# Attention's score matmuls in bursts of four, and the mixer's norms with squares added up on VectorE

## The reference

```python
u = rms_norm(h, norm_mix)
q, k, v, xl, gl = split(u @ w_in)            # 512 | 128 | 128 | 512 | 512 columns
q, k = rope(rms_norm(q)), rope(rms_norm(k))  # 8 query heads, 2 kv heads of 64
attn_out = softmax(q k^T / 8) v              # all 2048 keys, no mask
lru_out = (scan_forward + scan_backward)(conv(xl)) * gelu(gl)
mixed = concat(rms_norm(attn_out), rms_norm(lru_out))
h = h + mixed @ w_out
u = rms_norm(h, norm_ffn)
h = h + (silu(u @ w_gate) * (u @ w_up)) @ w_down    # 2816 wide
```

## Time and profile before

| | us |
|---|---|
| median of 3 runs | 2062.04 (2061.69 to 2065.15) |
| profiled execution, device time | 2065.6 |
| its span, slowest core (7) | 2064.1 |
| its span, fastest core (1) | 2040.4 |
| TensorE busy in it | 1836.4 |
| ScalarE / VectorE / GpSimd busy | 1070.5 / 933.8 / 348.9 |

### The profile page before, as it was taken

How to read it: one execution, slowest core, us unless ns; L and a number is a source line. 1 busy time by engine, 2 the same in 40 slices (tenths; PEclk the granted TensorE clock), 3 DMA queues, 4 the chain that set the end, 5 groups by cost and what they waited for, 6 DMA issues and landing times.

```text
span 2064.1 us, 24894 instructions; the slowest of 8 cores (2040.4 to 2064.1 us)
## 1 busy us (share of the span) xinstructions
PE 1836.4 (89%) x8272; PEld 727.3 (35%) x8272; DVE 933.8 (45%) x1159; ACT 1070.5 (52%) x1340; POOL 348.9 (17%) x380
## 2 busy tenths in 40 slices
PE   4994567865679999999999999999999999999998
PEld 1441223311112233333333344444444444444443
DVE  1666999856782221112141233353433534434331
ACT  3666888788988877877788711120211301213010
POOL 1223554445431122201000000000000000000000
PEclk9996778978889999999999999999999999999999
DMA  8653342481228465526642248567476575574632
GB/s 176 194 163 113 115 135 92 157 208 56 72 70 219 119 151 132 127 78 156 163 140 63 66 147 255 178 183 243 142 224 209 148 257 152 156 221 133 201 116 97
DMA packets 139784, 310.99 MB, mean 151 GB/s; under 512 B 18544, under 2 KB 26864, under 8 KB 139664
## 3 DMA queue, kind: packets, MB, share of 16 engines
q1 hardware_dynamic: 111632, 228.55, 37.9%
q0 software_dynamic: 28032, 80.86, 14.8%
HBM read 263.05 MB, written 69.99 MB: 161 GB/s over the span
## 4 chain that ended last, share of the span: by engine, by line
PE 69%; DVE 10%; DMA 9%; issue 5%; ACT 4%; POOL 2%; SPq 1%; DVEq 0%; POOLq 0%; ACTq 0%
PE ps_all L479 52%; PE ps_all L755 10%; PE ps_all L718 6%; DMA arena<-xT 2%; DVE arena L826 2%; DVE arena L790 2%; DMA arena<-rs_d 1%; DMA xl_d<-arena 1%; ACT arena L723 1%; DVE arena L572 1%; DMA arena<-xl_d 1%; DMA arena<-wd_s 1%; DMA arena<-w_out 1%; ACT arena L803 1%; DMA arena<-q_d 1%
## 5 line engine op out<-in xcount | busy, mean ns | idle before, releaser
L479 PE MATMUL ps_all<-arena 128*128 128x512 bf16 (+1 forms) x6224 | 1447.9, 379 | 149.1 <-ACT arena L803 27.3
L479 PEld LDWEIGHTS ps_all<-arena 128*128 128x128 bf16 x6224 | 609.1, 100 | 865.2 <-issue 262.0
L723 ACT ACTIVATE arena<-ps_all 128x1024 bf16<-128x1024 f32 x512 | 517.9, 1034 | 121.5 <-PE ps_all L755 102.5
L976 ACT ACTIVATE arena<-ps_all 128x512 f32<-128x512 f32 x176 | 104.6, 596 | 604.6 <-PE ps_all L479 604.3
L755 PE MATMUL ps_all<-arena 128*65 128x512 bf16 x1024 | 400.2, 408 | 6.4 <-DVE arena L731 6.3
L978 DVE SCALAR_TENSOR_TENSOR arena<-arena,ps_all 128x512 f32<-128x512 f32 x176 | 120.7, 687 | 365.2 <-ACT arena L976 364.5
L718 PE MATMUL ps_all<-arena 64*128 64x512 bf16 x1024 | 207.8, 402 | 63.2 <-ACT arena L723 57.3
L1001 POOL DMA_DIRECT2D outT<-arena x64 | 34.6, 540 | 997.0 <-DVE arena L999 996.4
L755 PEld LDWEIGHTS ps_all<-arena 128*65 128x65 bf16 x1024 | 107.8, 112 | 178.5 <-issue 133.0
L981 DVE SCALAR_TENSOR_TENSOR arena<-arena,ps_all 128x512 bf16<-128x512 f32 x176 | 120.9, 687 | 107.8 <-PE ps_all L479 104.6
L718 PEld LDWEIGHTS ps_all<-arena 64*128 64x128 bf16 x1024 | 51.2, 93 | 283.7 <-issue 283.7
(11 more groups left out here) (59 smaller groups left out, 894.6 us busy)
## 6 DMA issues: line engine op xcount, KB each, us to landing
arena<-wg_s SPq DMA_DIRECT2D x154, 256.0 KB, 3.0
arena<-wu_s SPq DMA_DIRECT2D x154, 256.0 KB, 2.9
arena<-wd_s SPq DMA_DIRECT2D x56, 704.0 KB, 5.8
arena<-xT SPq DMA_DIRECT2D x64, 512.0 KB, 7.1
outT<-arena POOLq DMA_DIRECT2D x64, 256.0 KB, 6.1
arena<-wo_s SPq DMA_DIRECT2D x56, 256.0 KB, 2.9
xl_d<-arena POOLq DMA_DIRECT2D x32, 256.0 KB, 3.6
gl_d<-arena POOLq DMA_DIRECT2D x32, 256.0 KB, 3.5
```

The source lines that it names most:

```text
L479: P.op("pe", lambda e: e.matmul(t.ap(n) if ap is None else ap(t), lhsT=lhsT, rhs=rhs, start=start, stop=stop), reads=reads, writes=[t], co ...
L723: P.op("act", lambda e: e.activation(out=pb, in_=T.ap(1024), func=AF.Exp, scale=0.125), reads=[T], writes=[("Pb", si % 3)], cost=c_act(102 ...
L976: P.op("act", lambda e, G=G, b=b: e.activation(out=tg[b], in_=G.ap(), func=AF.Tanh, scale=0.5), reads=[G], writes=[("tg", b)], cost=c_act( ...
```

## The change

Three things change.

- Attention: `emit_qk` takes a count m. With m = 2 it is one operation of four matmuls, into S0 and S1, that needs both PSUM tiles, and the two exponentials follow. In the first sequence this holds from step 192 on (`NS0`), in the second from its third step on. There are four `Pb` buffers for three.
- Norms of stage D: `sum_sq` squares in f32, adds the squares up on VectorE one after the other, the last sum in bf16, and one matmul with ones gives the sum over partitions. The buffers are now `hsq` (f32, two), `acc` and `accb` (one each), and `rf` has one buffer for two. The last addition of a chunk is written over h, which the store reads, instead of to a buffer `ot`.
- The planner: its costs for ScalarE, TensorE and DMA are others, it counts 0.1 us at each change between 64-row and other matmuls (`half`), and S0, S1 and O have one queue for both sequences.

```diff
-        q = P.bank_queue.setdefault((P.stream, kind), [])
+        q = P.bank_queue.setdefault((P.stream if kind == "m" else "B", kind), [])
...
+            if e == "pe":
+                if o["half"] != halved:
+                    cost += 0.1
+                halved = o["half"]
...
-                ch = 1 if o["eng"] == "pool" else 0
-                f = max(s + cost + 2.0, dma_free[ch]) + o["nbytes"] / 180e3
-                dma_free[ch] = f - 1.0
+                dma_free = max(s + cost + 0.9, dma_free) + o["nbytes"] / 200e3
+                f = dma_free + 1.2
...
-    return 0.04 + n / 1200.0 + 0.09 * ptrs
+    return 0.085 + n / 1200.0 + 0.09 * ptrs
...
-    return 0.0025 + n / 2400.0
+    return 0.006 + n / 2400.0
...
-                T = Bank(P, "S%d" % (si % 2), 2)
-
-                def both(e):
-                    for u in range(2):
-                        rows = slice(64 * u, 64 * u + 64)
-                        r = e.matmul(T.ap(1024)[:, u * 512:(u + 1) * 512], lhsT=kT[sq][rows, stl * 128:(stl + 1) * 128],
-                                     rhs=qb[n % 2][rows, :], start=True, stop=True)
+                T2 = [Bank(P, "S%d" % ((si + i) % 2), 2) for i in range(m)]
+
+                def burst(e):
+                    for i in range(m):
+                        for u in range(2):
+                            rows = slice(64 * u, 64 * u + 64)
+                            kt = (stl + i) * 128
+                            r = e.matmul(T2[i].ap(1024)[:, u * 512:(u + 1) * 512], lhsT=kT[sq][rows, kt:kt + 128],
+                                         rhs=qb[n % 2][rows, :], start=True, stop=True)
                     return r
-                P.op("pe", both, reads=[("k", sq, stl // 4), ("qb", n % 2)], writes=[T], cost=0.25, lat=0.25)
+                P.op("pe", burst, reads=[("k", sq, stl // 4), ("qb", n % 2)], writes=T2, cost=0.03 + 0.217 * m,
+                     lat=0.25, half=True)
...
-            for si in range(len(steps)):
+            emit_qk(0, 1)
+            emit_qk(1, 1)
+            for si in range(0, len(steps), 2):
+                two = si + 2 >= single
                 if si + 2 < len(steps):
-                    emit_qk(si + 2)
+                    emit_qk(si + 2, 2 if two else 1)
                 emit_pv(si)
+                if si + 2 < len(steps) and not two:
+                    emit_qk(si + 3, 1)
+                emit_pv(si + 1)
...
+        def sum_sq(N, parts, eng):
...
+            for n, (ap, key) in enumerate(parts):
+                sb = dc["s"] % 2
+                dc["s"] += n > 0
+                dst, dkey = (acc[a], ("acc", a)) if n == 0 else (hsq[sb], ("hsq", sb))
...
+                if n:
+                    o, okey = (accb[a], ("accb", a)) if n == last else (acc[a], ("acc", a))
+                    P.op("dve", lambda e, o=o, sb=sb: e.tensor_tensor(out=o, in0=acc[a], in1=hsq[sb], op=ALU.add),
+                         reads=[("acc", a), ("hsq", sb)], writes=[okey], cost=c_dve(512))
+            mm(N, ones_bf, accb[a], True, True, ["cm", ("accb", a)])
...
-            for k in range(8):
-                sb = dc["s"] % 2
-                dc["s"] += 1
-                P.op("act", lambda e, k=k, sb=sb: e.activation(out=hsq[sb], in_=h[:, k, :], func=AF.Square),
-                     reads=[("h", hb, k)], writes=[("hsq", sb)], cost=c_act(512), lat=0.25)
-                mm(N, ones_bf, hsq[sb], k == 0, k == 7, ["cm", ("hsq", sb)])
-            r = dc["r"] % 2
+            sum_sq(N, [(h[:, k, :], ("h", hb, k)) for k in range(8)], "act")
+            r = dc["r"] % len(rf)
```

83 lines of the change are left out of this document (43 added, 40 removed).

## The result

| | before | after |
|---|---|---|
| median of 4 runs each, us | 2062.28 (2061.69 to 2065.15) | 2010.62 (2007.97 to 2011.83) |
| ratio of the times, 95% interval | | 0.9745 (0.9728 to 0.9762) |
| span of the slowest core, us | 2064.1 | 2010.3 |
| mean over the cores: step 192 starts, us | 735.3 | 729.0 |
| last score pair | 1171.9 | 1206.5 |

A step's start is that of its first score matmul, and the matmuls of stage D are the helper's (line 483, 479 before) less the 1360 of stages A and C.

A forecast was written before the change was run, and what follows sets the result against it. TensorE was taken to bound the kernel, above 97% busy from some 700 us on. Terms -22.6 - 33.4 + 21 + 8 + 3 = -24 us took the profiled 2065.6 to 2041.6, less 3.6 for the median: 2038 us, range 2014 to 2058.

The forecast's parts named there:

- norms, 104 matmuls: Stage D: 16 ones-matmuls per chunk become 3, so 104 matmuls at 0.2178 us go, 22.6 us less.
- changes of shape, 159: Attention from step 192 on: 159 bursts each save one change of matmul shape and back, 0.21 us, 33.4 us less.
- waits, step 192 to 511: Attention bursts: TensorE waits 21 us for a 2.85 us ScalarE loop, plus 8 us for added changes of table.
- stage D's waits: Stage D: weights through GpSimd's queue, taken faster by D now, were costed at nothing, 0 us.
- up to step 192, matmuls of D credited: Before step 192: six more changes of table, two where ScalarE is full, cost +3 us, with 12 us allowed either way.
- I cost it at nothing: Stage D norms: a chain 2 to 5 us longer is covered by 38 us of down-projection or gate and up matmuls.
- TensorE's few waits from 745 us on: Old TensorE waits from 745 us on, 1.8 us of them for the exponential, were left as they are.
- 1225: Milestone: the last score pair comes near 1225 us for 1180.6, with 3621 helper matmuls behind it for 3998.
- A: Attention bursts: ScalarE's loop is longer than its parts, 3.2 us, and sets the pace; 2078 us; chance 0.09.
- B: Attention bursts: the second pair starts no closer than after a change of shape, nothing of 33.4 comes; 2060 us; chance 0.06.
- C: Attention from step 192: the loop is 2.8 us and the tables hide; -38, 2024 us; chance 0.18.
- D: First third: it loses 15 us or more by its new order; 2053 us and up; chance 0.09.

The follow-up runs named there:

- e1_norms: The kernel before with the change of the norms alone, old attention and old planner costs kept; ratio 0.9945 to the kernel before.
- e9_olddma: The changed kernel with the planner's old model of DMA time alone put back; ratio 0.9962 to the kernel before.
- e15_oldrear: The changed kernel planned with new costs up to step 96 of the first sequence and old ones from there; ratio 0.9836 to the kernel before.
- e13_oldnorms: The changed kernel with the old norms (16 ones-matmuls per chunk), bursts and planner costs kept; ratio 0.9856 to the kernel before.
- e5_pb4: The kernel before with a fourth probability buffer alone and one rstd buffer instead of two; ratio 1.0016 to the kernel before.
- e3_plan: The kernel before with the planner's new costs and common bank queue alone, old attention and norms; ratio 0.9977 to the kernel before.
- e7_pb3: The changed kernel with three probability buffers instead of four; ratio 0.9895 to the kernel before.
- e14_oldfront: The changed kernel planned with old costs up to step 96 of the first sequence and new ones from there; ratio 0.9772 to the kernel before.
- e6_exp768: The changed kernel, same queues, with each attention exponential doing 768 of the 1024 columns; ratio 0.9661 to the kernel before.

## Why the prediction was wrong

The account of the 52.1 us on the mean core, beside the forecast:

| term | forecast | measured |
|---|---|---|
| norms, 104 matmuls | -22.6 | -22.5 |
| changes of shape, 159 | -33.4 | -35.6 |
| waits, step 192 to 511 | +21 + 8 | +19 |
| stage D's waits | 0 | -4.2 |
| up to step 192, matmuls of D credited | +3 | -9.8 |
| not explained, behind step 511 | | +1 |
| sum | -24 | -52 |

(From step 192 to 511: +40.8 = 266 more matmuls of D x 0.2165 - 159 x 0.224 + 18.8. The waits counted one by one give 31.1 - 11.4 = 19.7, 1 more. Behind: -86.6 = 386 fewer matmuls x 0.2165, 4.2 of waits, 1.2 the other way. Up to step 192: -6.3, with 16 more matmuls of D done.)

Three terms failed, and all to the same side: what moves before step 192 (13 us of the 28 missed), the waits of the bursts (10) and stage D's waits (4); the changes of shape add 2.

**Norms.** Right in size. VectorE got 13 x 0.692 and, for its 8 squares, 0.789 us with f32 out where 0.447 was: 11.7 us per chunk for 11. (Both are means that a few long ones raise. The middle one of the 64 squares on core 0 takes 0.683 us, four take 1.5 to 2.8; before it was 0.42. So a square costs 0.26 more, near the 0.24 taken, and the 0.69 taken for it holds.) The cover of the chain holds in the changed kernel: the view names 0.6 us of waits behind the additions. It fails in three kernels with old costs: 3.3 us in e1_norms, 5.3 in e9_olddma, 2.9 in e15_oldrear. So "I cost it at nothing" came out right by the planner's edit, which the forecast had not weighed for it, and not by the 38 us of matmuls that it named; that is luck.

**Bursts, what they take away.** Right: the second pair starts 0.215 to 0.228 us behind the first in all 159 places of core 0, and a change and back costs 0.224 for the 0.21 taken.

**The wait they add, and the tables.** The mechanism was right: the loop is 2.73 to 2.79 us for 2.85, and a change of table adds up to 1.2 to it. The sum was too high by 10 us in three ways. The loop's waits are 16 us for 21: 2.85 for 2.79 makes up 3 to 4 of these 5. The seven changes of table cost 6 us for 8, since some fall in intervals that are long already. And the step that left out the old waits was wrong: "TensorE's few waits from 745 us on, 1.8 us of them for the exponential, I leave as they are". They were 10 to 13 us up to the last score pair, and 7 to 10 us are left beside the loop's and the tables', so some 3 us of the old waits now lie within these. The view hides this, as it counts only what lies behind a matmul's modelled end; starts show the rest. That the total of 31 is near the forecast's 21 + 8 is luck, since the 31 hold the old waits as well.

The forecast's milestones did not agree with its sum either: 1225 + 3621 x 0.2178 + 9 = 2023 us for the core whose sum gives 2064 - 24 = 2040. Its own terms put the last score pair near 1234 (1180.6 + 3 + 252 x 0.2165 - 33.4 + 29), so the 1225 does not follow from them, and I had not set the one against the other.

**Before step 192.** "+3 us" was -9.8, the largest part of the miss. This is the step that failed most: the six more changes of table were counted (65 for 59 before step 96, as forecast), and what new costs and a fourth buffer do to the order was put at nothing with 12 us either way. The experiments show how far this stretch goes with the queues alone: step 192 starts anywhere from 720 us (e13_oldnorms, cores 0 to 3) to 753 (e9_olddma). With D's matmuls counted, the fourth buffer alone gains 3 us there (e5_pb4) and the planner's edits alone nothing (e3_plan); taken out of the changed kernel, the buffer is worth 5 (e7_pb3) and the new costs up to step 96 are worth 6 (e14_oldfront). So both have a part in it, together and not each by itself. Two stretches of core 0 in the changed kernel, steps 0 to 64 and 64 to 96 (columns as above):

```profile
405.80:517.30 111.50, 79.03 (x283) 21.09 (x282) 63.30 (x44) 101.97 (x113) 43.67 (x32) 0.79 0.51 137
517.30:598.90 81.60, 48.39 (x155) 12.59 (x155) 73.71 (x56) 73.16 (x83) 35.47 (x14) 0.73 0.21 63
```

And before:

```profile
402.70:543.10 140.40, 85.22 (x296) 21.95 (x297) 86.51 (x59) 122.84 (x140) 71.37 (x44) 0.76 0.46 122
543.10:604.60 61.50, 41.38 (x148) 10.86 (x148) 46.20 (x38) 59.24 (x67) 22.73 (x9) 0.83 0.24 67
```

The same 64 steps take 29 us less (25 on the mean core) with 27 fewer instructions on ScalarE, 14 of them tanh of the recurrent branch, and 20 of these us (19) come back in the next 32 steps, with 16 more instructions. So that branch was moved between attention's steps, and what is left is the difference of two large terms. Which of the moved pieces makes it is open.

**Stage D.** "I cost that at nothing too", of the weights, missed 4 us: waits for `wd_s` were there before (4.3 us on core 0), and by the view the kernels planned with the new DMA formula there have 0.4 to 1.9 us of them on the mean core, those with the old one 2.3 to 7.4. They stand in the waits view from the last score pair on, and the forecast took from that view only the row for the exponential.

**The rivals.** A falls by the loop of 2.79 us and by e6_exp768; B by the rows of four. C, with a loop of 2.8 us, is close on the loop and has the right sign, but 2024 us is still 13 too high, and its tables do not hide: 6 us are there. D's mechanism was there, the first third by its new order, with the other sign.

## What to carry to other kernels

Price the old waits of a stretch before adding new ones, since a new one can cover some of them, count both by the distances between starts, and set the sum of terms against the milestones that the same terms give. Where a planner draws the queues, the parts of a change are not additive: its costs decide whether weights and sums come in time, and here one formula for DMA and one constant for ScalarE were worth 36 and 26 us on the mean core, in a kernel whose operations stayed the same. And where one engine's burst feeds another, let the consumer be signalled behind the first piece: this took 0.21 us out of the loop and gave 9 us (8 on the mean core) without a change in the order of any queue.

## What the runs showed of the hardware

A square of 512 columns from bf16 to f32 took 0.683 us on VectorE in the middle (0.789 on average, with four long ones) where bf16 to bf16 took 0.42 (0.447), and an addition of f32 operands 0.69. A change from 128-row to 64-row matmuls and back cost TensorE 0.224 us, and a second pair on 64 rows each followed the first at 0.215 to 0.228 us in all 159 places of core 0, about the 0.2165 of one full matmul. From the end of an exponential to the start of the burst that waited for it lay 0.14 us, and from a score pair's start to the exponential on it 0.43 or 0.49.
